# Logarithms on ScalarE, and head sums, roots and reciprocals on columns in a fused four-stage block

## What is computed

```
# a: gated linear recurrence, its rate needs softplus(-lam), lam of 256 numbers
log_a = -LRU_C * r * softplus(-lam);  a = exp(log_a)
b = sqrt(-expm1(2.0 * log_a)) * (i * u);  h = scan(a, b)

# b: attention of 8 heads with a forget term
log_f = log_sigmoid(f_logit + f_bias)             # [272, 8]
c = cumsum(log_f);  s = q k^T / 8 + (c_q - c_k);  p = softmax(s)

# c: recurrent group, 4 heads of 64
kk = heads(k * k_k)
kk = kk / maximum(sqrt(sum(kk * kk, axis=-1)), 1e-12)      # one sum per head and token
S = S * w_t - (S kk_t) (kk_t * a_t) + v_t k_t;  o_t = S r_t # over 272 tokens, in chunks of 64
mean = mean(o);  var = mean((o - mean)**2)                  # per head and token
o = (o - mean) * rsqrt(var + GN_EPS) * ln_w + ln_b
out = (o + bonus) * g
```

## Time and profile before

| | us |
|---|---|
| median of 3 runs | 966.58 (965.36 to 966.65) |
| the profiled execution | 964.8 |
| its span | 963.1 |
| TensorE busy | 920.6 (96%) |
| VectorE busy | 701.9 (73%) |
| ScalarE busy | 517.9 (54%) |
| GpSimd busy | 232.7 (24%) |
| mixer (start to its last output tile) | about 0 to 214 |
| feed-forward, layer 0, layer 1 | the rest |

### The profile page before, as it was taken

The page is one execution under the profiler, slowest core; times in us unless marked ns, Lnnn a source line. Parts: engine busy times, 40 slices in busy tenths (PEclk is TensorE's granted clock), DMA queues, the critical chain, the costliest instruction groups (busy, mean ns, idle before and its releaser), DMA issues.

```text
span 963.1 us, 19384 instructions
## 1 busy us (share of the span) xinstructions
PE 920.6 (96%) x7806; PEld 848.2 (88%) x7806; DVE 701.9 (73%) x1087; ACT 517.9 (54%) x934; POOL 232.7 (24%) x194
## 2 busy tenths in 40 slices
PE   4999998798999999989999999999899999999997
PEld 4787897688999998879999899999699999999995
DVE  6899566458898997476878675577658778655684
ACT  6543456345665565374756465444655665555443
POOL 3344512243121221002412040033022212310250
PEclk9999998898999999999999999999999999999999
DMA  8443220043555555538444526555374434645451
GB/s 312 132 132 110 68 68 25 1 154 112 194 177 187 184 176 184 187 108 314 158 154 147 181 86 207 187 184 189 117 288 154 132 132 148 203 153 187 165 189 52
DMA packets 41560, 150.18 MB, mean 156 GB/s; under 512 B 4608, under 2 KB 4864, under 8 KB 41216
## 3 DMA queue, kind: packets, MB, share of 16 engines
q1 hardware_dynamic: 39456, 141.54, 44.3%
q10 hardware_dynamic: 2016, 7.41, 2.1%
HBM read 147.88 MB, written 1.05 MB: 155 GB/s over the span
## 4 chain that ended last, share of the span: by engine, by line
PE 87%; DVE 7%; DMA 2%; ACT 1%; issue 1%; POOL 0%; ACTq 0%; DVEq 0%; SPq 0%
PE ps L724 85%; PE ps L1019 1%; DVE wlo L1634 1%; DMA gts<-in_g 1%; PE ps L1122 0%; DMA raw<-in_ws 0%; DVE rw_pi L1739 0%; DVE S L1634 0%; DVE xa L2028 0%; DVE rw_pe L1859 0%; DVE pcraw L1634 0%; DVE fS L1634 0%; ACT whi L1233 0%; ACT L1233 0%; DVE ht L1642 0%
## 5 line engine op out<-in xcount | busy, mean ns | idle before, releaser
L1233 ACT ACTIVATE whi<-raw 128x1024 fp32r<-128x1024 f32 (+1 forms) x264 | 278.0, 1055 | 308.5 <-PE ps L724 301.0
L724 PE MATMUL ps<-xh,whi 128*128 128x256 f32 (+2 forms) x1408 | 406.0, 288 | 18.7 <-ACT xh L1233 13.2
L1634 DVE TENSOR_TENSOR wlo<-raw,whi 128x1024 fp32r<-128x1024 f32 (+1 forms) x256 | 325.1, 1275 | 114.8 <-ACT whi L1233 113.9
L724 PE MATMUL ps<-xl,whi 128*128 128x256 f32 (+2 forms) x1408 | 399.9, 284 | 4.9 <-DVE xl L1642 4.9
L724 PE MATMUL ps<-xh,wlo 128*128 128x256 f32 (+2 forms) x1408 | 399.0, 283 | 0.0
L724 PEld LDWEIGHTS ps<-xh,whi 128*128 128x128 f32 x1408 | 266.9, 190 | 26.4 <-issue 22.0
L724 PEld LDWEIGHTS ps<-xl,whi 128*128 128x128 f32 x1408 | 266.5, 189 | 6.2 <-DVE xl L1642 5.8
L724 PEld LDWEIGHTS ps<-xh,wlo 128*128 128x128 f32 x1408 | 267.5, 190 | 0.0
L2241 POOL TENSOR_TENSOR gts<-gts 128x256 f32<-128x256 f32 x32 | 35.7, 1125 | 144.8 <-DVE gts L1642 144.2
L724 PE MATMUL ps<-yh,whi 128*128 128x256 f32 x232 | 65.3, 282 | 0.0
L724 PE MATMUL ps<-whi,xh 128*128 128x512 f32 (+1 forms) x152 | 61.1, 402 | 4.3 <-DVE kT L1634 1.7
(11 more groups left out here) (339 smaller groups left out, 1320.9 us busy)
## 6 DMA issues: line engine op xcount, KB each, us to landing
raw<-in_ws SPq DMA_DIRECT2D x262, 512.0 KB, 3.8
h<-in_rel ACTq DMA_DIRECT2D x2, 1024.0 KB, 14.0
qc<-in_gam ACTq DMA_DIRECT2D x3, 512.0 KB, 4.3
mt<-in_m ACTq DMA_DIRECT2D x2, 576.0 KB, 6.5
h<-in_hT SPq DMA_DIRECT2D x4, 272.0 KB, 5.7
gts<-in_lng ACTq DMA_DIRECT2D x2, 512.0 KB, 8.5
out<-ht SPq DMA_DIRECT2D x4, 256.0 KB, 2.0
gts<-in_g ACTq DMA_DIRECT2D x2, 448.0 KB, 10.7
```

What stands on the lines that cost most here:

```text
L724: return e.matmul(o, l, r, start=start, stop=stop, skip_group_check=True)
L1233: return e.activation(o, a, f, bias=bias, scale=scale, accum_out=acc)
L1634: return e.tensor_tensor(o, a, b, op)
```

## The change

**Logarithms.** Both series of 13 operations go. ScalarE, after its absolute value and exponential, takes one more activation, Ln with a bias of one. The factors in `fo.sum` and `la.c` change from 2 to 1 and from 8 to 4, since the series gave half the logarithm. `la.a` on ScalarE moves from before the entry to between `in 0 7` and `inend 0`.

**Head sums.** `head_sums` makes the squares the stationary side and two columns of `bones` the moving one: three matmuls of two columns, in blocks of 128 tokens that overlap, give 128x6 with tokens on partitions. Root, maximum and reciprocal act on 128x6 or 128x12 (`kroot`, `oroot`). ScalarE then copies the six columns out to 128x384, 64 copies of each (`widen`), and three matmuls with the identity lay them back with features on partitions (`over_heads`). VectorE multiplies straight from PSUM. This holds for the unit keys (`rw.norm`, `rw.root`, `rw.unit`) and for the output norm (`rw.var`, `rw.oi`, `rw.fin`); the means stay as they are.

**Orders.** The strings of the mixer and of both layers are new on all four engines; the feed-forward's are the same. What matters for the prediction, on TensorE in the mixer: C6, C7 come ahead of `rw.wa 0`; `rw.wa 1` and `rw.gup` move behind six of the eight `tok` steps; `rw.X` moves from between the `tok` steps to behind tiles (0,2) and half of (1,2). From the last tiles on the order is

The diff, without the strings and with the unchanged neighbours cut:

```diff
+KN = [(0, 128), (128, 128), (192, 128)]
+ON = [(0, 128), (128, 128), (144, 128)]
...
-              ("rw.pm",), ("rw.unit",), ("rw.wa", 1), ("rw.ka",), ...
+              ("rw.pm",), ("rw.root",), ("rw.unit", 0), ("rw.unit", 1), ("rw.wa", 1), ("rw.ka",), ...
-           ("rw.fin", 0), ("rw.fin", 1)],
+           ("rw.oi", 0), ("rw.oi", 1), ("rw.fin", 0), ("rw.fin", 1)],
-        "f": [("fo.proj",)] + [("fo.log", n) for n in range(3)] + [("fo.sum",), ("fo.lr",)],
+        "f": [("fo.proj",), ("fo.log",), ("fo.sum",), ("fo.lr",)],
-        "n": [("la.a",), ("la.b", 0), ("la.b", 1), ("la.c",)],
+        "n": [("la.a",), ("la.c",)],
...
+        kroot = sb("kroot", [128, 2, 3, 2])
+        oroot = sb("oroot", [128, 2, 3, 2])
+        wide = [two(n)[:, 0:384] for n in ("Y", "XT")]
...  TensorE
+            def head_sums(ps, x, blocks):
+                for b, (t0, n) in enumerate(blocks):
+                    t = mm(ps[:, 2 * b:2 * b + 2], x[:, t0:t0 + n], bones[:, 0:128:64], True, True)
+                return t
+            def over_heads(ps, m, blocks):
+                done = 0
+                for b, (t0, n) in enumerate(blocks):
+                    t = mm(ps[:, done:t0 + n], wide[m][:, half(b, 128)], ident[:, done - t0:n], True, True)
+                    done = t0 + n
+                return t
             def rw_norm(m):
-                mm(ps[:, 0:TP], bones, B6["pe"][:, m, :], True, True).then_inc(*pe.says(("rw.pkn", m)))
+                head_sums(ps, B6["pe"][:, m, :], KN).then_inc(*pe.says(("rw.pkn", m)))
+            def rw_unit(m):
+                pe.wait_ge(("rw.kx", m), ("d.c0",))
+                over_heads(ps, m, KN).then_inc(*pe.says(("rw.pkb", m)))
             def rw_var(m):
-                mm(ps[:, 0:T], bones, B6["pe"][:, m, 0:T], True, True).then_inc(*pe.says(("rw.pvar", m)))
+                head_sums(ps, B6["pe"][:, m, 0:T], ON).then_inc(*pe.says(("rw.pvar", m)))
+            def rw_fin(m):
+                pe.wait_ge(("rw.ox", m))
+                over_heads(ps, m, ON).then_inc(*pe.says(("rw.pob", m)))
...  ScalarE
-                act(B6["pi"][:, m, :], ps_of(("kn", m))[:, 0:TP], ACT.Sqrt).then_inc(
+                act(kroot[:, m, :, :].rearrange("p b e -> p (b e)"), ps_of(("kn", m))[:, 0:6], ACT.Sqrt).then_inc(
+            def widen(root, m):
+                o = wide[m].rearrange("p (a c) -> p a c", c=64)
+                return act(o, root[:, m, :, :]....unsqueeze(2).to_broadcast([128, 6, 64]), ACT.Copy)
+            def rw_unit(m):
+                sc.wait_ge(("rw.kr",))
+                widen(kroot, m).then_inc(*sc.says(("rw.kx", m)))
+            def rw_fin(m):
+                sc.wait_ge(("rw.oi", m))
+                widen(oroot, m).then_inc(*sc.says(("rw.ox", m)))
+                sc.wait_ge(("fo.e",), ("c.ones",))
+                act(la[2], la[1], ACT.Ln, bias=ones[0:8, 0:1]).then_inc(*sc.says(("fo.l",)))
+                sc.wait_ge(("lr.e",), ("c.ones",))
+                act(lam4[:, 1, :], lam4[:, 0, :], ACT.Ln, bias=ones[:, 0:1]).then_inc(*sc.says(("lr.l",)))
...  VectorE
-                ts(two("pi"), two("pi"), 1e-12, MAX).then_inc(*d.says(("rw.kmx",)))
-                e.reciprocal(two("pi"), two("pi")).then_inc(*d.says(("rw.kr",)))
-                tt(two("kk"), two("kk"), two("pi"), MUL).then_inc(*d.says(("rw.kk",)))
+                ts(k, k, 1e-12, MAX).then_inc(*d.says(("rw.kmx",)))          # k = kroot, 128x12
+                e.reciprocal(k, k).then_inc(*d.says(("rw.kr",)))
+            def rw_unit(m):
+                d.wait_ge(("rw.pkb", m), ("rw.k0", m), ("rw.sq", m))
+                tt(B6["kk"][:, m, :], B6["kk"][:, m, :], ps_of(("kb", m))[:, 0:TP], MUL).then_inc(
-                e.reciprocal(q, q).then_inc(*d.says(("rw.oi", m)))            # q = rw_pe, 128x272
-                tt(o, o, q, MUL).then_inc(*d.says(("rw.on", m)))
+                e.reciprocal(q, q).then_inc(*d.says(("rw.oi", m)))            # q = oroot, 128x6
+                tt(o, o, ps_of(("ovb", m))[:, 0:T], MUL).then_inc(*d.says(("rw.on", m), frees=("ovb", m)))
-            def log1p(name, v, part, after):
...
-                stt(x, s, -2.0, x, MUL, ADD).then_inc(*d.says(("fo.f",)))
+                stt(x, s, -1.0, x, MUL, ADD).then_inc(*d.says(("fo.f",)))
-                stt(o, lam4[:, 1, :], 8.0, o, MUL, ADD).then_inc(*d.says(("lr.sp",)))
+                stt(o, lam4[:, 1, :], 4.0, o, MUL, ADD).then_inc(*d.says(("lr.sp",)))
```

More of the change, by code:

```diff
@@ L1216, in tensor @@
             do = {"in": enter, "inend": lambda st: squares(st, 7), "cols": columns,
-                  "tile": tile, "tok": tokens, "rw.wa": rw_wa, "rw.gup": rw_gup, "rw.norm": rw_norm,
+                  "tile": tile, "tok": tokens, "rw.wa": rw_wa, "rw.gup": rw_gup, "rw.norm": rw_norm, "rw.unit": rw_unit, "rw.fin": rw_fin,
                   "rw.bonus": rw_bonus, "rw.M": rw_M, "rw.X": rw_X, "rw.leva": rw_leva, "rw.levb": rw_levb,
@@ L1616, in scalar @@
             do = {"init": init, "split": split, "in": enter, "inend": enter_end, "init2": init2, "rw.lora": rw_lora,
[L1617 removed]
+                  "rw.wa": rw_wa, "rw.gup": rw_gup, "rw.kk": rw_kk, "rw.norm": rw_norm, "rw.unit": rw_unit, "rw.fin": rw_fin, "rw.pm": rw_pm, "rw.pi": rw_pi, "rw.P": rw_P, "rw.pe": rw_pe,
                   "rw.leva": rw_leva, "rw.pair": rw_pair, "rw.o": rw_o, "rw.mean": rw_mean, "rw.var": rw_var,
@@ L1990, in late @@
                     *d.says(("ob.lo", g, 0)))
-            def rate(part):
-                log1p("lr.l", [lam4[:, i, :] for i in range(4)], part, ("lr.e",))
             def rate_end():
@@ L2218, in vector @@
                   "res": residual, "shift": shift, "mix": shift_mix, "rw.tg2": rw_lora, "rw.wa": rw_wa, "rw.scan": rw_scan,
-                  "rw.k": rw_k, "rw.unit": rw_unit, "rw.pe": rw_pe, "rw.al": rw_al, "rw.be": rw_be, "rw.rh": rw_rh,
+                  "rw.k": rw_k, "rw.root": rw_root, "rw.unit": rw_unit, "rw.pe": rw_pe, "rw.al": rw_al, "rw.be": rw_be, "rw.rh": rw_rh,
                   "rw.ki": rw_ki, "rw.rk": rw_rk, "rw.bonus": rw_bonus, "rw.M": rw_M, "rw.X": rw_X, "rw.lb": rw_lb,
                   "rw.levb": rw_levb, "rw.pair": rw_pair, "rw.scanU": rw_scanU, "rw.scanS": rw_scanS,
-                  "rw.mean": rw_mean, "rw.fin": rw_fin, "rw.oc": rw_oc, "fo.proj": fo_proj, "fo.log": fo_log,
-                  "fo.sum": fo_sum, "fo.lr": fo_lr, "at": attend, "late": late, "la.a": lambda: rate(0),
-                  "la.b": lambda n: rate(n + 1), "la.c": rate_end, "lr.conv": lr_conv, "lr.exp": lr_exp,
+                  "rw.mean": rw_mean, "rw.oi": rw_oi, "rw.fin": rw_fin, "rw.oc": rw_oc, "fo.proj": fo_proj,
+                  "fo.sum": fo_sum, "fo.lr": fo_lr, "at": attend, "late": late, "la.c": rate_end, "lr.conv": lr_conv, "lr.exp": lr_exp,
                   "lr.tan": lr_tan, "lr.b": lr_bb, "lr.scan": lr_scan, "xya": xya, "qk": qk, "op": out_tile,
```

110 lines of the change are left out of this document (47 added, 63 removed).

## The result

| | us, median | lowest to highest |
|---|---|---|
| before | 966.6 | 965.4 to 967.5 (6 runs) |
| after | 956.55 | 953.7 to 959.2 (6 runs) |
| ratio | 0.990 | 95%: 0.988 to 0.992 |

The change is 10.0 us where 4.5 were forecast; 956.55 lies inside the range of 955 to 966, near its lower end. Two later series of the same kernel gave 956.0 each, and those of the kernel before 965.9 to 966.7. The profiled execution of the kernel after is the fastest of its series (953.65 us, span 951.9), so its 11.2 us against the span of before (963.1) are somewhat more than the rule.

The account below looks back on a forecast made before the run. Bound by the entry, VectorE from 30 to 65 us, full TensorE to 140, then the recurrent chain's tail. -7.0 + 4.7 to the last tile, -3.9 at scanU0, -0.6 in the scan: -4.5, 962.1 us; range 955 to 966.

Parts of the forecast that it names:

- Entry, -4.5: Kernel start: with the rate's logarithm moved away, TensorE's second matmul starts near 8.5 instead of 13.02 us, 4.5 us earlier.
- the entry's end: Root and next tile after the entry: one weight split less, 1.2 us, against 0.7 for table loads; gives 0.5 us.
- Rival 4: Root at the entry's end: each table change costs twice its load row, 3.2 us lost, 965.3 us; chance 0.03.
- VectorE-paced stretch, -7.0 at the token steps: 30 to 65 us: TensorE wins 2.0 us of waits; with 4.5 and 0.5 from before, token steps come 7.0 us early.
- the rest of the 13 us is cover, not gain: Same stretch: some 13 us leave VectorE, but TensorE can win no more than its 2.0 us of waits.
- Dense part, +4.7: Token steps to last tile, TensorE full: work moved in costs its full length, net +4.7 us; last tile ends at 138.0.
- Rival 1: Chain behind the entry comes late, `rw.X` stalls TensorE 1.5 to 4 us, more behind it: up to 969.1 us; chance 0.12.
- The scan, -0.6: Recurrence's scan: f1.4, 1.2 us, leaves from between the steps, half of it hidden by the scan's latency; 0.6 us won.
- Norm and output tiles, 0 with -3.6 and +2: Behind the scan: reciprocals removed but later mean1 and hand-overs added; counted 0, bounds -3.6 and +2 us.
- Clock, 0: Granted clock behind 150 us: no gain in the forecast's sum; only rival 3 counted 1.6 us for it.
- rival 3: Tail: norm's chain keeps its 3.6 us, denser scan keeps the clock, 1.6 us; 9.7 us in all, 956.9; chance 0.17.
- Layers, 0: Layers 0 and 1: TensorE full, moved attention steps bring no work or new operands; 0, bounds -1.5 and +2 us.

## Why the forecast was right in place and wrong in size

- **Entry, -4.5: right** in the trace (-4.6), and the three loads cost what the load's row said: the root starts at 21.09, 4.3 us earlier, and the next tile 5.4 (24.95), so the entry's end gave 0.8 where 0.5 was forecast. Rival 4 is out.
- **VectorE-paced stretch, -7.0 at the token steps: -8.5** (65.19 to 56.68). Some 1.0 of it is TensorE's work that changed sides and not time won: `rw.wa 1` and `rw.gup` (1.1 and 1.0) now run behind this mark, `fo.lr` (1.1) ahead of it. Like with like it is -7.5, near the forecast. But "the rest of the 13 us is cover, not gain" does not hold for the new order: there the single pieces undone cost 6.8 and 5.8 us. That the sum came near all the same is in part luck, since the forecast asked neither what the new order needs of that cover nor what a wait in this stretch does to the clock.
- **Dense part, +4.7: right.** The last tile ended 2.9 us earlier where 2.3 were forecast: 8.5 less 4.7 and less the 1.0 that came over. ScanU 0 is 4.8 us earlier where 3.9 were forecast. Rival 1 is out: `rw.X` starts at 83.66 without a wait.
- **The scan, -0.6: the step that failed.** It got 3.3 us shorter in the profile of after. The forecast took the scan to lose one step, f1.4, and counted half of that as hidden by the scan's latency. But TensorE ran H, f1.4 and f2.3 in the first step without a wait, so nothing of f1.4 was hidden. H, which the forecast itself had counted into the dense part, left the scan as well, and f2.3 moved behind scanS 1. Nor did it look at what leaves on VectorE: with its steps put back there the scan is 14.2 us long all the same (some 1.3 of it the half clock in f2.3's transposes), and with H and f1.4 put back 12.7. Both lists had to be thinned for the 10.6.
- **Norm and output tiles, 0 with -3.6 and +2: mis-sized.** From the last scan matmul to the final root it is 49.3 us before, 47.3 in the first profile of after and 50.0, at half clock, in the third. In the new kernel the norm is worth 2.2 us by the medians, `late 1` 3.2. The forecast named `late 1`'s new place and the wait at 189.21 behind it, and then let the tile's k = 7 decide, so that k = 2 to 5, which now run ahead of the group's last split (179.16, the wait for k = 6 at 182.16), were given nothing.
- **Clock, 0:** rival 3 came closest in time (956.9), and both parts of its mechanism are there in some measure. From scanU 0 to the end of the last scan matmul the granted clock went from 0.89 (151.32 to 165.97 us) to 1.00 (146.56 to 157.64) in the first and the third profile of after, and to 0.86 in the second; but behind scanU 1, where before lost its clock, the net gain is 0.2 us with f2.3 moved in, so what the clock gave of the rival's 1.6 is not separated. (From 151 to 166 us by the clock on the wall it fell from 0.89 to 0.77, since the next group of matmuls stands there now.) The norm kept 2.2 of its 3.6 us. The half-clock stretch in the output tiles of before (0.57 from 190 to 194 us) is gone in the profile of after and in part back in its third series.
- **Layers, 0: right** for their order. Behind the final root the profiles of after are 0.8 to 1.1 us shorter than that of before, within what single profiles of all these kernels scatter.

Where the missing 5.5 us are, by the profile of the third series of after, whose time of 956.65 is near the median: scanU 0 0.9, scan 2.7, from the last scan matmul to the final root -0.7 at half clock (2.0 in the first series at full clock), behind it 0.8. That is 3.7; the remaining 1.8 are the profile of before, which lies that much under its median.

## What to carry to other kernels

A move is priced on every engine's list, between the same two steps, and not on that of one engine alone. In a chain bound by latency the longest list between two steps sets the step: here 3.0 us of VectorE's work cost the chain 2.2 us where TensorE's list was short, and 2.4 us of TensorE's work cost it 2.0. The same work of TensorE, moved ahead of the scan where that engine is full, cost 2.6. An order and the arithmetic that it was laid out for are one change: here each alone lost 3 to 8 us, and two moves that were worth 3 to 6 us in the new kernel cost 4 in the old. What a removed instruction is worth is asked of the order that will stand. And a wait of 3 to 5 us in a full stretch was not the whole price: in each such case here the next 4 to 9 us ran at half clock.

## What the hardware showed that was not expected

- Two executions of one program, equal to 0.1 us for 170 us, then ran the same 9 us at clocks of 1.00 and 0.53. The Trainium skill (TensorE: Matmul & The Clock Gate, Part 1) says that the gate's observation is free-running and that the change differs between runs of one kernel; the two traces differ in that way, here in the middle of the kernel, and do not show why.
- VectorE's reciprocal cost by what lies along the free dimension, not by how much there is: 128x640 4.15 us, 128x272 and 8x272 1.85 and 1.84, 128x12 0.23, 128x6 0.19. To put the long side on partitions cost, for each half of the output norm, head sums of 0.73 us, a copy of 0.50 and a lay-back of 0.84, on TensorE and ScalarE.
- Exponential and logarithm took a table load each (16.68 and 18.19), though the Trainium skill (ScalarE: Activation LUTs, Table sets) has a set with both. Nor are the 2.66 us for a switch seen that the same page has (What ACT_TABLE_LOAD costs): 1.28 is all, with the next activation 0.01 us behind.
